# Last feed-forward: gate and up of 18 of 22 tiles by seven products of block sums in place of eight block products

## What is computed

```
h = adaln_in(s, g_pre, m, i)
y = (jax.nn.silu(h @ w_gate) * (h @ w_up)) @ w_down
x = x + 0.5 * m_gate * rmsnorm(y, g_post)
```

## Time and profile before

| what | value |
|---|---|
| median of 3 runs | 2354.3 us (2354.18 to 2357.28) |
| span of the profiled execution | 2357.0 us |
| PE busy | 2290.3 us, 97% of the span |
| DVE busy | 1309.0 us, 56% |
| ACT busy | 901.3 us, 38% |
| POOL busy | 128.7 us, 5% |
| mean granted TensorE clock | 0.993 |

### The profile page before, as it was taken

One profiled execution on the slowest core, in us unless ns is written; L12 is line 12 of the kernel. 1 busy time (PEld: TensorE's weight loads), 2 busy tenths in 40 slices (PEclk: granted clock), 3 DMA queues, 4 the chain that ended last, 5 costly groups with the idle time before them and its releaser, 6 DMA issues.

```text
span 2357.0 us, 30952 instructions
## 1 busy us (share of the span) xinstructions
PE 2290.3 (97%) x11832; PEld 1893.4 (80%) x11832; DVE 1309.0 (56%) x1903; ACT 901.3 (38%) x1363; POOL 128.7 (5%) x250
## 2 busy tenths in 40 slices
PE   7999999999999999999999999999989999999998
PEld 2688888889987877888888788888877777888887
DVE  5777375575567555833266557533366965432334
ACT  1543222544544564433222452223264425322232
POOL 1011010000021000000011001000010000000000
PEclk9999999999999999999999999999999999999999
DMA  9688365355552110233358338532332312333222
GB/s 359 212 289 296 122 234 174 127 157 184 161 167 82 50 46 13 87 125 107 108 191 282 107 100 289 182 116 89 116 118 94 103 49 86 98 99 113 93 89 72
DMA packets 97789, 329.33 MB, mean 140 GB/s; under 512 B 16033, under 2 KB 16449, under 8 KB 96642
## 3 DMA queue, kind: packets, MB, share of 16 engines
q1 hardware_dynamic: 67810, 224.39, 28.4%
q0 software_dynamic: 28848, 101.99, 13.1%
q10 hardware_dynamic: 1008, 1.25, 0.1%
HBM read 315.77 MB, written 8.40 MB: 138 GB/s over the span
## 4 chain that ended last, share of the span: by engine, by line
PE 86%; DVE 6%; ACT 4%; issue 2%; DMA 1%; SPq 0%; DVEq 0%; ACTq 0%; POOLq 0%; POOL 0%; PEldq 0%
PE psum L601 20%; PE psum L603 20%; PE psum L602 20%; PE psum L852 5%; PE psum L854 5%; PE psum L853 5%; PE psum L661 2%; DVE w_lo L2072 1%; PE psum L1364 1%; PE psum L1347 1%; PE psum L942 1%; ACT w_hi L1403 1%; PE psum L943 1%; PE psum L944 1%; ACT square L1896 1%
## 5 line engine op out<-in xcount | busy, mean ns | idle before, releaser
L601 PE MATMUL psum<-h_hi,w_hi 128*128 128x512 f32 (+1 forms) x2092 | 786.2, 376 | 11.2 <-DVE w_lo L2072 4.9
L603 PE MATMUL psum<-h_hi,w_lo 128*128 128x512 f32 (+1 forms) x2092 | 778.0, 372 | 0.0
L602 PE MATMUL psum<-h_lo,w_hi 128*128 128x512 f32 (+1 forms) x2092 | 777.6, 372 | 0.0
L2072 DVE TENSOR_TENSOR w_lo<-raw,w_hi 128x1024 fp32r<-128x1024 f32 (+2 forms) x400 | 454.8, 1168 | 258.6 <-ACT w_hi L1403 252.9
L1403 ACT ACTIVATE w_hi<-raw 128x1024 fp32r<-128x1024 f32 (+2 forms) x394 | 384.1, 1006 | 302.8 <-PE psum L854 232.7
L601 PEld LDWEIGHTS psum<-h_hi,w_hi 128*128 128x128 f32 x2092 | 394.6, 189 | 85.6 <-issue 10.2
L603 PEld LDWEIGHTS psum<-h_hi,w_lo 128*128 128x128 f32 x2092 | 394.5, 189 | 69.0
L602 PEld LDWEIGHTS psum<-h_lo,w_hi 128*128 128x128 f32 x2092 | 394.7, 189 | 66.8 <-issue 1.0
L2241 DVE TENSOR_TENSOR prod<-psum,square 128x512 f32<-128x512 f32 (+1 forms) x110 | 70.1, 638 | 372.1 <-PE psum L603 324.3
L1443 ACT ACTIVATE act_hi<-prod 128x512 fp32r<-128x512 f32 (+3 forms) x110 | 64.8, 589 | 500.1 <-DVE prod L2241 500.1
L852 PE MATMUL psum<-w_hi,act_hi 128*128 128x512 f32 x528 | 206.2, 390 | 1.3 <-DVE w_lo L2072 1.3
(11 more groups left out here) (374 smaller groups left out, 2438.3 us busy)
## 6 DMA issues: line engine op xcount, KB each, us to landing
raw<-in_gate_up SPq DMA_DIRECT2D x220, 512.0 KB, 4.4
mod_raw<-in_w_rows POOLq DMA_DIRECT2D x152, 512.0 KB, 5.2
raw<-in_down_rows SPq DMA_DIRECT2D x66, 512.0 KB, 4.2
raw<-in_down_a SPq DMA_DIRECT2D x32, 384.0 KB, 3.7
raw<-in_hy_in SPq DMA_DIRECT2D x24, 512.0 KB, 3.6
raw<-in_mix_in SPq DMA_DIRECT2D x22, 512.0 KB, 4.3
raw<-in_down_b SPq DMA_DIRECT2D x32, 320.0 KB, 3.2
mod_raw<-in_w_mod POOLq DMA_DIRECT2D x16, 512.0 KB, 8.4
```

The source lines that it names most:

```text
L601: pe.matmul(out, w_hi[:, slot, c:c + P], hi, start=start, stop=False)
L602: pe.matmul(out, w_hi[:, slot, c:c + P], lo, start=False, stop=False)
L603: return pe.matmul(out, w_lo[:, slot, c:c + P], hi, start=False, stop=stop)
L2072: ins = dve.tensor_tensor(w_lo[:, slot, 0:cols], raw[:, slot, 0:cols], w_hi[:, slot, 0:cols].bitcast(F32), ALU.subtract)
```

## The change

Of the last feed-forward's 22 tiles, all but the first four are computed another way: pairs 5 to 12 of `ffns[4][0]` and all ten of `ffns[4][2]`. A pair is a product of a 2 x 2 matrix of weight blocks (gate and up, each cut into its first and last four k) with a 2 x 2 matrix of input blocks (first and last four k, first and last 256 tokens). It was eight block products; it becomes seven, of sums of blocks (the Winograd form of Strassen's scheme). Each product has four k, three matmuls each, of 256 columns.

Three of the weight operands are sums that have to be made for each pair, and one is a sum of a sum: GpSimd makes the four of them (`tees`). The seven operands of 128 x 512, called grains, are split by ACT (`grain_high`) and DVE (`grain_low`) into eight half slots of the old ring. The four sums of input blocks are made once by DVE (`make_sum`) and split once (`sum_high`, `sum_low`). Five products stay in their PSUM banks or are joined to one by accumulation, and the rest is added up by one ACT copy and five DVE additions of 256 columns for each pair. `h_piece` gives `piece` a full place for each piece, which the input sums are made from. The diff, cut to its core:

```
+FAST_BANK = (0, 1, 2, 3, 0, 2, 3)
+FAST_OPENS = (0, 1, 2, 3)
+U2, U3, C22, C21, C12 = 1, 2, 3, 4, 5
+T1, T2, T3, T4 = 1, 2, 3, 4
+SUM_OF = {1: 1, 2: 2, 3: 0, 6: 3}
+SUM_TURN = {1: 0, 2: 1, 0: 2, 3: 3}
+SUM_MADE = {2: 1, 0: 2, 1: 3, 3: 4}
...
+    ffns[4][0].fast, ffns[4][2].fast = 8, 0
+    ffns[4][1].after_fast, ffns[4][3].after_fast = ffns[4][0], ffns[4][2]
...
+            sums = y[:].rearrange("p (n a) (b c) -> p n (a b) c", n=4, c=CTX)
+            u2 = [full[:, 0, 0:CTX], full[:, 0, CTX:SEQ]]
+            tee1, tee2 = full[:, 1, :], sumsq[:, :]
+            grain_hi_at = w_hi[:].rearrange("p r (a c) -> p (r a) c", a=2)
+            grain_lo_at = w_lo[:].rearrange("p r (a c) -> p (r a) c", a=2)
...
+        def fast_tiles(j):
+
+            if j in SUM_OF:
+                return sum_tiles(SUM_OF[j])
+            k, c = {0: (0, 0), 4: (4, 0), 5: (4, CTX)}[j]
+            return h_hi[:, k:k + 4, c:c + CTX], h_lo[:, k:k + 4, c:c + CTX]
+
+        def grain_slot(s, i, j):
+
+            return (2 * (s.fast_first() % RING) + 7 * i + j) % GRAINS
...
+        def wait_used(eng, s, i, j):
+
+            if j == 6:
+                eng.wait_ge(block_done, RING + s.fast_first() + 2 * i + 2)
+            else:
+                eng.wait_ge(grain_done, ONCE + 6 * (s.pairs_before + i) + j + 1)
+
+        def wait_slot_free(eng, s, i, j):
+
+            g = 7 * i + j
+            if g < GRAINS:
+                eng.wait_ge(block_done, s.fast_first() + g // 2 + 1)
+            else:
+                wait_used(eng, s, *divmod(g - GRAINS, 7))
...
+        def grain_source(s, i, j):
+
+            b = s.fast_first() + 2 * i
+            gate, up = raw[:, b % RING, :], raw[:, (b + 1) % RING, :]
+            return (gate[:, 0:512], tee2, up[:, 0:512], tee1, gate[:, 512:1024], gate[:, 0:512], up[:, 512:1024])[j]
...
+            def fast_pair(s, i, p0):
+
+                n, b = s.pairs_before + i, s.fast_first() + 2 * i
+                for j in range(7):
+                    if j < 5:
+                        pe.wait_ge(grain_lo, ONCE + 5 * n + j + 1)
+                    else:
+                        pe.wait_ge(lo_split, RING + b + j - 4)
...
+                    if j in FAST_OPENS and i == 0:
+                        pe.wait_ge(result_read, p0 + j + 1)
+                    elif j == 0:
+                        pe.wait_ge(gate_read, ONCE + n)
+                    elif j in FAST_OPENS:
+                        pe.wait_ge(fast_read, ONCE + 5 * (n - 1) + (0, U2, C21, C12)[j])
+                    elif j == 4:
+                        pe.wait_ge(kept_first, ONCE + n + 1)
+                    else:
+                        pe.wait_ge(fast_read, ONCE + 5 * n + (U3 if j == 5 else C22))
+                    hi, lo = fast_tiles(j)
+                    out, g = psum[:, (p0 + FAST_BANK[j]) % 4, 0:CTX], grain_slot(s, i, j)
+                    joins = j not in FAST_OPENS
+                    for k in range(4):
+                        w = slice(k * P, k * P + P)
+                        pe.matmul(out, grain_hi_at[:, g, w], hi[:, k, :], start=(not joins and k == 0), stop=False,
+                                  skip_group_check=joins)
+                        pe.matmul(out, grain_hi_at[:, g, w], lo[:, k, :], start=False, stop=False, skip_group_check=joins)
+                        ins = pe.matmul(out, grain_lo_at[:, g, w], hi[:, k, :], start=False, stop=(k == 3), skip_group_check=joins)
...
+            def grain_high(s, i, j):
+
+                grain_made(act, s, i, j)
+                wait_slot_free(act, s, i, j)
+                act.activation(grain_hi_at[:, grain_slot(s, i, j), :], grain_source(s, i, j),
+                               ACT.Copy).then_inc(hi_split if j >= 5 else grain_hi, 1)
...
+                for i in range(end):
+                    n, a = s.pairs_before + i, (s.fast // 2 + i) % 2
+                    ahead_of(i, 0)
+                    if i:
+                        keep(i - 1)
+                    act.wait_ge(grain_done, ONCE + 6 * n + 1)
+                    if n >= 2:
+                        act.wait_ge(fast_read, ONCE + 5 * (n - 2) + C12)
+                    act.activation(u2[n % 2], psum[:, p0 % 4, 0:CTX], ACT.Copy).then_inc(kept_first, 1)
+                    for j in range(1, 5):
+                        ahead_of(i, j)
+                    act.wait_ge(grain_done, ONCE + 6 * n + 5)
+                    act.activation(silu[:, a, 0:CTX], psum[:, p0 % 4, 0:CTX], ACT.Silu).then_inc(gate_read, 1)
+                    ahead_of(i, 5)
+                    act.wait_ge(fast_read, ONCE + 5 * n + C21)
+                    act.activation(silu[:, a, CTX:SEQ], silu[:, a, CTX:SEQ], ACT.Silu).then_inc(silu_ready, 1)
+                    ahead_of(i, 6)
+                keep(end - 1)
...
+            def make_sum(n):
+
+                if n == 2:
+                    dve.tensor_tensor(sums[:, 2], h_front[:, 0:4, :], h_back[:, 0:4, :], ALU.subtract).then_inc(sum_made, 1)
+                elif n == 0:
+                    dve.tensor_tensor(sums[:, 0], h_back[:, 0:4, :], h_back[:, 4:8, :], ALU.add).then_inc(sum_made, 1)
+                elif n == 1:
+                    dve.wait_ge(sum_made, ONCE + SUM_MADE[0])
+                    dve.tensor_tensor(sums[:, 1], sums[:, 0], h_front[:, 0:4, :], ALU.subtract).then_inc(sum_made, 1)
+                else:
+                    dve.wait_ge(sum_made, ONCE + SUM_MADE[1])
+                    dve.tensor_tensor(sums[:, 3], h_front[:, 4:8, :], sums[:, 1], ALU.subtract).then_inc(sum_made, 1)
...
+                def product(i):
+                    n, f = s.pairs_before + i, s.fast // 2 + i
+                    a = f % 2
+                    dve.wait_ge(block_done, RING + s.fast_first() + 2 * i + 2)
+                    dve.tensor_tensor(prod[:, a, 0:CTX], psum[:, (p0 + 3) % 4, 0:CTX], u2[n % 2], ALU.add).then_inc(fast_read, 1)
+                    dve.wait_ge(silu_ready, f0 + i + 1)
+                    dve.wait_ge(fast_read, ONCE + 5 * n + C12)
+                    dve.tensor_tensor(prod[:, a, :], prod[:, a, :], silu[:, a, :], ALU.mult).then_inc(result_read, 2)
...
+                for i in range(end):
+                    n, a = s.pairs_before + i, (s.fast // 2 + i) % 2
+                    if i:
+                        product(i - 1)
+                    ahead_of(i, 0)
+                    if i:
+                        keep(i - 1)
+                    ahead_of(i, 1)
+                    dve.wait_ge(grain_done, ONCE + 6 * n + 2)
+                    dve.wait_ge(kept_first, ONCE + n + 1)
+                    dve.tensor_tensor(u2[n % 2], psum[:, (p0 + 1) % 4, 0:CTX], u2[n % 2], ALU.add).then_inc(fast_read, 1)
+                    ahead_of(i, 2)
+                    dve.wait_ge(grain_done, ONCE + 6 * n + 3)
+                    dve.wait_ge(fast_read, ONCE + 5 * n + U2)
+                    dve.tensor_tensor(u3[:, :], psum[:, (p0 + 2) % 4, 0:CTX], u2[n % 2], ALU.add).then_inc(fast_read, 1)
+                    ahead_of(i, 3)
+                    dve.wait_ge(grain_done, ONCE + 6 * n + 4)
+                    dve.wait_ge(fast_read, ONCE + 5 * n + U3)
+                    dve.tensor_tensor(prod[:, a, CTX:SEQ], psum[:, (p0 + 3) % 4, 0:CTX], u3[:, :], ALU.add).then_inc(fast_read, 1)
+                    ahead_of(i, 4)
+                    ahead_of(i, 5)
+                    dve.wait_ge(grain_done, ONCE + 6 * n + 6)
+                    dve.tensor_tensor(silu[:, a, CTX:SEQ], psum[:, (p0 + 2) % 4, 0:CTX], u2[n % 2], ALU.add).then_inc(fast_read, 1)
+                    ahead_of(i, 6)
+                product(end - 1)
+                keep(end - 1)
...
                 for n in range(5, 2 * KT):
+                    low_piece(n, kept)
+                    if kept and n == 12:
+                        make_sum(2)
+                if kept:
+                    for n in (0, 1, 3):
+                        make_sum(n)
...
+            def tees(s):
+
+                for i in range(s.fast_pairs()):
+                    n, b = s.pairs_before + i, s.fast_first() + 2 * i
+                    gate, up = raw[:, b % RING, :], raw[:, (b + 1) % RING, :]
+                    for m in (b, b + 1):
+                        pool.wait_ge(raw_landed[m % RING], 16 * (m // RING + 1))
+                    if n:
+                        pool.wait_ge(grain_lo, ONCE + 5 * (n - 1) + 4)
+                    else:
+                        pool.wait_ge(sum_made, ONCE + 4)
+                    pool.tensor_tensor(tee1, up[:, 0:512], gate[:, 0:512], ALU.subtract).then_inc(tee_ready, 1)
+                    pool.wait_ge(tee_ready, ONCE + 4 * n + T1)
+                    pool.tensor_tensor(tee2, up[:, 512:1024], tee1, ALU.subtract).then_inc(tee_ready, 1)
+                    pool.tensor_tensor(up[:, 0:512], up[:, 512:1024], up[:, 0:512], ALU.subtract).then_inc(tee_ready, 1)
+                    pool.wait_ge(tee_ready, ONCE + 4 * n + T3)
+                    pool.wait_ge(grain_lo, ONCE + 5 * n + 1)
```

(55 more changed lines are left out.)

142 lines of the change are left out of this document (127 added, 15 removed).

## The result

| kernel | median | range | runs |
|---|---|---|---|
| before | 2355.02 us | 2354.18 to 2357.28 | 4 |
| after | 2368.81 us | 2365.73 to 2370.46 | 4 |

The changed kernel is slower: ratio 1.0055, 95% interval 1.0041 to 1.007, that is 9.7 to 16.5 us. The forecast was 2370 us with the range 2340 to 2386. The profiled execution has a span of 2366.5 us (before 2357.0) and took 2368.14 us.

What follows compares the result with a forecast made beforehand. TensorE was taken to bound the kernel unless made to wait, as VectorE and GpSimd taking turns would do. 14.9 us for the pairs plus 0.9 for the input sums, on 2354.3, gave 2370 us, range 2340 to 2386.

Steps and rivals of the forecast that it cites:

- TensorE, 10.08 a pair: TensorE in each changed pair: 84 matmuls of 256 columns at 0.120 us, 10.08 us where it took 10.88.
- In turns: VectorE's two-SBUF-input instructions and GpSimd's subtractions each wait for the other's whole instruction; pair 11.71 us, chance 0.60.
- The reason given: Inferred from VectorE's one-input and two-input times: two inputs use two reading ways, so GpSimd must find its own.
- GpSimd's price, 0.97: One GpSimd subtraction of 512 columns, four a pair: 0.97 us, between bounds 0.54 and 1.41.
- The pair, 11.71: One pair: 4 x 0.97 GpSimd, 6.24 two-input VectorE, 1.27 uncovered additions, 0.32 handovers; 11.71 us against 10.88.
- the second rival: VectorE's list too long without GpSimd's hindrance if it often waits for ScalarE; decides from 2.5 us of waits, chance 0.07.
- Eighteen pairs: All changed pairs of the last feed-forward: 18 x (11.71 - 10.88) = 14.9 us more.
- The input sums, 0.9: Three input sums on VectorE delay the first product and block five's start: 0.9 us more.
- Side by side: GpSimd and VectorE don't hinder each other; pair 10.08 us, 13.5 us gained, 2341 us, chance 0.30.
- VectorE late by itself: VectorE's list too long without turns, through waits for ScalarE; three more waits would give 11.6 and 2368 us, chance 0.07.
- The half pace: TensorE's 256-column matmuls at half the 512-column time, 9.52 us a pair, nobody late; 2331 us, chance 0.03.
- The whole: Sum over the kernel: 14.9 for the pairs and 0.9 for the sums, 15.8 us more.

Runs made afterwards that it cites:

- experiment 2: The changed kernel with VectorE's low grains of all pairs but the first of each half reading PSUM instead of SBUF, GpSimd's subtractions kept: 2342.13 us.
- experiment 5: The changed kernel with GpSimd's four subtractions of each pair replaced by fills, which write SBUF and read nothing: 2345.14 us.
- experiment 6: The kernel before, with 40 GpSimd subtractions of 512 columns in the down stage in the middle of the last feed-forward: 2354.2 us, one execution.
- experiment 8: The changed kernel with only T1 of GpSimd's four subtractions of each pair computed, the other three left out: 2344.86 us.
- experiment 4: The changed kernel with each of GpSimd's four subtractions of a pair replaced by a copy of 512 columns, one SBUF input: 2340.82 us.
- experiment 1: The changed kernel with GpSimd's four subtractions of each pair left out, semaphores and all else as they were: 2342.71 us.

## Why the prediction came out

**TensorE, 10.08 a pair: right.** 0.120 us a matmul held in every run where nobody was late.

**In turns: right, and shown** by experiments 2, 5 and 6, though a subtraction holds VectorE off for 1.17 of its 1.31 us and not for the whole instruction. The reason given, that two inputs take both reading ways, fits a copy and a fill too, but the runs show only who holds whom, not why.

**GpSimd's price, 0.97: too low.** 1.30 us long, 1.17 as VectorE feels it; within the bounds 0.54 to 1.41. (The Trainium skill, GPSIMD Engine Reference, section Elementwise — side-by-side cycle accounting, by a quarter of its figure: 1.12, an estimate; nearer than mine.)

**The pair, 11.71 against 11.88: nearly right, by errors that cancel.** The working charged all four subtractions, 4 x 0.97 = 3.88, where VectorE loses 3.10: T3 runs at a time when VectorE adds from PSUM and then waits for ScalarE, and parts of T1 and T4 pass under its other instructions. At the right price all four would have made 4.68. On VectorE's side the working had 6.24 + 1.27 + 0.32 = 7.83 where its list takes 8.78. Its instructions follow each other at 0.60 and 0.34 us, not at the 0.693 and 0.422 that each lasts, which makes it shorter; but it does all five additions, and waits 1.00 us for the seventh high grain, which ScalarE has in its list behind the silu that needs the C21 addition. That wait was named under the second rival and left out of the sum.

**Eighteen pairs: the step that was mis-sized.** TensorE's wait falls in 14 of 18 pairs. A steady pair did cost 1.00 us more than before (0.83 forecast), but a pair without a wait gives back 0.80. In the last pair of each half GpSimd has no sums to make, and only one block split stands among VectorE's additions ahead of u3. In the second half T1 to T3 of the second pair are made while the down stage still runs (2181.94 to 2185.86) and VectorE is idle, and the first wait is in the third pair; the first half's first one is only 0.38. So 18 x 0.83 = 14.9 became 5.00 + 5.03 = 10.03. The working had one steady period and no start and end.

**The input sums, 0.9: 0.71,** and block five started at 2011.20, not near 2012.7; all that came ahead of it in this execution was earlier by 1.3.

**The whole.** +10.7 from the profile's stages for a forecast of +15.8, and +13.8 timed. Single executions lie up to 6 us off their kernel's median (2340.28 for 2344.86 in experiment 8, 2346.79 for 2340.82 in experiment 4), so the 3 us between 10.7 and 13.8 belong to no step. The sign and the mechanism were right; the forecast's nearness to the median, 1.2 us, is luck in good part: its sum was 5.1 us above what the stages show, and the medians came out 3.1 further apart than the stages.

**The rivals.** Side by side, forecast 2341, is what experiments 1 and 2 show with the turns taken away: 2342.7 and 2342.1. VectorE late by itself is refuted by experiment 1. The half pace is refuted by 0.120.

## What to carry to other kernels

An idle GpSimd is not free help for VectorE: while it reads SBUF, each VectorE instruction with two SBUF inputs queues behind it, and a subtraction that would have taken VectorE 0.69 us cost it 0.91 to 1.13 us of waiting when GpSimd made it (T4, T1, T2). Where VectorE is near the bound, do the work on VectorE, in the places where it waits for another engine, or give GpSimd what needs no reading, or let VectorE read one input from PSUM. When an engine's list is close to the bound, count the slack first (here 1.30 us of 10.08) and then what holds it up: below the slack nothing was lost here, above it everything was.

## What the runs showed of the hardware

A VectorE instruction of 512 columns with two SBUF inputs lasts 0.69 us, but the next starts 0.60 after it; one of 256 with an input in PSUM lasts 0.41 and the next starts after 0.34. A GpSimd subtraction of 512 columns takes 1.30 us, a copy 0.62, a fill 0.53. A GpSimd copy with one input holds VectorE off as a subtraction does, for a shorter time. TensorE waiting 1.6 us in every 11.88 kept its granted clock of 1.00.
